# Third attention: value matrices as the stationary operand, two heads in the column halves of the array, probabilities scaled before they are turned

## The chip, the core and the metric

The program runs on one core of a Trainium2 chip. The core has five engines that run side by side, each in the order of its own instructions: TensorE (PE in the profile, with its weight loads as PEld), VectorE (DVE), ScalarE (ACT), GpSimd (POOL) and SyncE (SP, which only issues transfers here). They wait for each other by semaphores. The metric is the time of one execution in microseconds (us), as the median of several runs.

## The reference, cut to what matters

Two transformer blocks run one after the other on 256 tokens of width 1024. The change lies in the second block, in its mixer: 16 heads of width 64 in four groups of four (`moba`, `nsa`, `diff`, `swa`), each a softmax attention over 256 tokens with its own mask and slopes.

```python
p = _masked_softmax(sc, mask, sink)          # moba, slc, win, swa: one map for each head
o = jnp.einsum('bgrnqk,bgnkd->bgrnqd', p.astype(vb.dtype), vb)
...
return gates[..., 0:1] * o_c + gates[..., 1:2] * o_s + gates[..., 2:3] * o_w      # nsa
...
p = _masked_softmax(s1, mask) - lam * _masked_softmax(s2, mask)                   # diff
...
mix = jnp.concatenate([_merge(o_moba), _merge(o_nsa), _merge(o_diff), _merge(o_swa)], axis=-1)
x = x + _rms_norm(mix @ w_out[l], attn_post_norm[l])
```

At 256 tokens the selected and the windowed attention of `nsa` see all keys, so both are plain causal maps (`slc` and `win`). Everything is float32.

## The kernel before

**Matrix products with weights.** Weights arrive as float32 in slabs of two units (`raw`, three slabs). One unit is eight blocks of 128x128. Each unit is split into a high part (`wh`, rounded to fp32r) and a low part (`wl` = `raw` - `wh`), and a product is three fp32r matmuls. `MADE` gives each unit a letter that says who makes its parts: `d` low on VectorE and high on ScalarE, `p` low on GpSimd and high on ScalarE, `v` both on VectorE, `q` low on GpSimd and high on VectorE. A unit is made (`split`) some four units ahead of its use.

**Order.** All engines walk one list of steps, `ORDER`, and each issues only what it has to do in a step. The string `MIX["maps"]` weaves the third attention into the matrix products that it lies beside: a dot takes the next piece of the main chain (the projections `nkc`, `nq`, `d`, `s`, `mq`, `mk` of the second block, then the product `out2` with `w_out_2` in units `down`), a letter the next step of a job. Jobs are `a` (compressed keys and values), `b` and `c` (`slc` and `win`, by pairs of heads), `d` to `g` (the `df` maps), `h` and `i` (`swa`), `j` and `k` (`moba`).

**One pair of heads.** `scores` puts the two score maps side by side on the array, in its row halves. `score` (VectorE) adds the bias and takes the maximum, `exp` (ScalarE) makes unnormalised probabilities and their sums in a tile of `ringP` (seven tiles). `p_turn` transposes a map in three pieces of 128x128 on TensorE and ScalarE copies the 384 columns to a tile of `ringT` (five tiles). In `value` the turned probabilities are stationary and the 64 columns of V stream. `apart` does each of the three products in two column halves of the array: six instructions of 64 columns for one head. `o_out` (VectorE) multiplies the output by 1/sum (and by the gate for `nsa`) as it leaves PSUM, into `OM2`, token by head. For `nsa`, `cmp_value` multiplies the compressed probabilities `PcT` with their values, and VectorE adds.

**Joins.** Eight steps `join` transpose `OM2` back in two pieces of 128x128 each, and ScalarE (high) and VectorE (low) put the result into `mi`, the input of `out2`. `out2` reads `mi` in the order `KORD2` = 2, 3, 4, 5, 6, 7, 0, 1; the last four are in its `tail`. The `df` maps (`diff`) go through `d_mix`, `value`, `d_out`, `d_norm` and joins 4 and 5.

**Banks.** PSUM has eight banks; the steps of the attention take theirs in turn from five (`B5`). Every call of a matmul is issued by line 528, a transpose by 531, ScalarE by 534, VectorE by 537 to 555, GpSimd's copies by 564, transfers by 567.

Of the kernel before, what the change touches and what calls it, by code (L numbers as in the profile page):

```python
# [21 lines left out]
NUNREAD = 13  # L22
NBASE = 4
# [190 lines left out]
def segments():  # L214
# [163 lines left out]
    for n in range(2):  # L378
        jobs.append(two(("swa", n)) + ([("join", 6), ("join", 7)] if n else []))
    for n in range(2):  # L380
        jobs.append(two(("moba", n)) + [("join", n)])
# [27 lines left out]
    def names(steps):  # L409
# [12 lines left out]
        "ddvvvdvdppdpdppvvpdqpdpqvddpvpdvpdddvpdvpdvdddvqdddqqpddpddqddvdddddddpvvvdppvpppdvvddddqdvddddd"  # L422
        "dddddddddvdddvdpqpdddddddqddddddddddddddppddpddddddqddddvddvdvddddddpdvvdddvdvdddddd")
MIX = {
    "scan": "..abc.aabc..bb.c..ab.bc...a.b.b..cc...bcb.c..a..cc...bc.b.ca.bbcd.c..cbcbad.bd.c.e.b.ecf.ef.f.f.f",
    "latent": "..a......aaaaaaaa................bc....b.fgc.b..f.c.g..de.b.cf...d.gf.e.hi.dg.h.e.d..ie.h..i.h..i",
    "out1": "............c.caac..aaacabab.bbaaaaaa.baaabbbcbbbbbbbbccc....",
    "ffn1": "..aaaaac..acaba......aaaaaaaa....bbbbccbb......b.bbbb...bbbb............",
    "maps": "...a.....acbabcbc..cc.bbb.ede.eed.ecag.agcdgcggadc.b.bfcgbefdc.ab.dgfbe.dbhffbbhhhfa.ccccf.igecbeif."
            "gahf.ddib.b.bbigchijbjj..cbhcibchkhajkhcikkhcjbiijbcijkijkcijg.kjjkk.ggkkij.k.",  # L430
# [27 lines left out]
LAST_JOIN = [s for s in ORDER if s[0] == "join"][-1]  # L458
# [124 lines left out]
def program(nc, dr):  # L583
    ctx = ExitStack()
    with ctx:  # L585
# [184 lines left out]
        OM2 = fa(o, 2048).rearrange("p (c n) -> p c n", c=2); o += 2048  # L770
        PcT, VC = fa(o, 256), fa(o + 256, 256); o += 512
        ringP = [fa(o + 384 * i, 384) for i in range(7)]; o += 7 * 384
        ringT = [fa(o + 384 * i, 384) for i in range(5)]; o += 5 * 384
# [30 lines left out]
        HEAD = dict(moba=0, slc=4, win=4, df1=8, swa=12)  # L804
# [13 lines left out]
        for m, i in p_slot.items():  # L818
            p_prior[m] = at_p.get(i - 7)
        for m, i in t_slot.items():  # L820
            t_prior[m] = at_t.get(i - 5)
# [8 lines left out]
        def Pm(m):  # L830
            return ringP[p_slot[m] % 7]

        def Tm(m):
            return ringT[t_slot[m] % 5]
# [23 lines left out]
        def opened(e, u):  # L858
# [6 lines left out]
            elif PLACE[u] >= NBASE and OPENS[1] <= u < OPENS[1] + NWIDE - NBASE:  # L865
                e.wait_ge(*pe.at(LAST_JOIN))

# [14 lines left out]
        def tensor(e):  # L882
# [53 lines left out]
            for step in ORDER:  # L936
# [356 lines left out]
                elif kind == "p_turn":  # L1293
# [3 lines left out]
                    e.wait_ge(*(dve.at(("d_mix", m_[1])) if m_[0] == "df1" else act.at(("exp", m_))))  # L1297
# [3 lines left out]
                elif kind == "value":  # L1301
# [8 lines left out]
                    apart(b[:, 64:128], PT[:, 256:384], V[1], start=False).then_inc(*pe.up(step))  # L1310
                elif kind == "join":
# [4 lines left out]
                    for c in range(2):  # L1316
                        m = e.transpose(b[:, 128 * c:128 * c + 128], OM2[:, c, 128 * kt:128 * kt + 128], ident)
# [15 lines left out]
                elif kind in ("o_out", "d_out"):  # L1333
                    banks.give(("value", a[0] if kind == "o_out" else ("df1", a[0])))
# [18 lines left out]
                elif kind == "cmp_turn":  # L1353
# [4 lines left out]
                    m.then_inc(*pe.up(step))  # L1358
                elif kind == "cmp_value":
                    n, = a  # L1360
                    b = bank(step, B5)
                    e.wait_ge(*act.at("cmp_turn"))
                    e.wait_ge(*dve.at("cmp_kv"))
                    for c in range(2):
                        m = e.matmul(b[:, 128 * c:128 * c + 128], PcT[:, 128 * c:128 * c + 128], VC[:, 128 * n:128 * n + 128],
                                     start=True, stop=True)
# [3 lines left out]
        def scalar(e):  # L1370
# [3 lines left out]
            for step in ORDER:  # L1374
# [268 lines left out]
                elif kind == "p_turn":  # L1643
                    m_, = a
                    e.wait_ge(*pe.at(step))
                    if t_prior[m_]:
                        e.wait_ge(*pe.at(("value", t_prior[m_])))
# [843 lines left out]
```

## Time and profile before

| | us |
|---|---|
| median of 3 runs | 898.12 (897.7 to 898.27) |
| the profiled execution, its own time | 897.94 |
| span of its instructions | 896.1 |
| TensorE busy | 884.4 (99%) |
| TensorE weight loads busy | 782.7 (87%) |
| VectorE busy | 667.4 (74%) |
| ScalarE busy | 466.3 (52%) |
| GpSimd busy | 200.4 (22%) |

The page shows the clock of TensorE as full in all 40 slices. The chain that ended last is 96% TensorE. A busy figure of TensorE is not its peak: the end of a matmul is modelled, some 0.2 us after its last column went in, so short waits between matmuls are covered by the tail of the matmul before. What a step costs TensorE is therefore read from starts: from the start of its first row to the start of the next row of another kind. A fp32 matmul shows as two records (two passes), a transpose as one, a fp32r matmul as one. In a row of the trace, `128*64 128x64` is a stationary operand of 128 rows and 64 columns and a moving one of 64 columns.

### The profile page before, as it was taken

Reading aid. Unit: us, or ns where it says so; the run is one execution under the profiler, and the core shown is the slowest. Engines: PE = TensorE matmul, PEld = TensorE weight load, DVE = VectorE, ACT = ScalarE, POOL = GpSimd, SP = SyncE. Lnnn points to the kernel's source line nnn. Section 1 sums busy time; section 2 is a strip of 40 time slices with the busy share of each in tenths; the row PEclk is TensorE's granted clock in tenths of the full one; section 3 lists DMA queues with packets and bytes.
Section 4 is the critical chain, followed back from the end, with each engine's and each line's share of the span. In section 5 each row is a group of like instructions: output and inputs, shape, how many; then the busy total and the mean of one; then the engine's idle time right before and its main releaser. Section 6 shows DMA issues by size and latency. Waiting matters only on the chain.

```text
span 896.1 us, 16529 instructions
## 1 busy us (share of the span) xinstructions
PE 884.4 (99%) x6641; PEld 782.7 (87%) x6641; DVE 667.4 (74%) x1253; ACT 466.3 (52%) x940; POOL 200.4 (22%) x113
## 2 busy tenths in 40 slices
PE   9999999999999999999999999999999999999997
PEld 8879999989999798888888899977888888888886
DVE  7745987586447877786666767768888788788885
ACT  7444336665344774444444657866553545543443
POOL 4123421531132120553214522230001111210100
PEclk9999999999999999999999999999999999999999
DMA  8356453153424746555564374215354465465441
GB/s 331 114 184 234 140 174 112 48 212 142 142 96 145 278 163 236 188 196 187 187 219 169 124 247 165 97 48 211 142 222 161 182 213 204 152 230 188 174 156 48
DMA packets 23180, 153.66 MB, mean 171 GB/s; under 512 B 2864, under 2 KB 3248, under 8 KB 5568
## 3 DMA queue, kind: packets, MB, share of 16 engines
q1 hardware_dynamic: 22384, 150.44, 46.8%
q0 software_dynamic: 576, 2.10, 0.6%
q8 instruction: 53, 0.87, 0.4%
q14 instruction: 23, 0.19, 0.1%
q10 hardware_dynamic: 144, 0.07, 0.0%
HBM read 151.28 MB, written 1.05 MB: 170 GB/s over the span
## 4 chain that ended last, share of the span: by engine, by line
PE 96%; DVE 2%; ACT 1%; issue 1%; DVEq 0%; ACTq 0%
PE pb L528 94%; PE pb L531 2%; ACT FA L534 1%; DVE FA L537 0%; DVE wl L537 0%; ACT R L534 0%; DVE X L543 0%; DVE wh L552 0%; DVE FA L546 0%; ACT wh L534 0%; DVE FA L540 0%; DVE st L540 0%; DVE st L555 0%; DVEq L585 0%; DVE FA L543 0%
## 5 line engine op out<-in xcount | busy, mean ns | idle before, releaser
L528 PE MATMUL pb<-R,wh 128*128 128x256 f32 (+2 forms) x2224 | 545.5, 325 | 3.3 <-DVE R L543 2.0
L528 PE MATMUL pb<-R,wl 128*128 128x256 f32 (+1 forms) x1512 | 420.0, 281 | 0.0
L528 PEld LDWEIGHTS pb<-R,wh 128*128 128x128 f32 x2224 | 369.5, 188 | 43.3 <-ACT R L534 3.4
L537 DVE TENSOR_TENSOR wl<-raw,wh 128x1024 fp32r<-128x1024 f32 (+1 forms) x207 | 273.3, 1344 | 76.6 <-ACT wh L534 74.8
L537 POOL TENSOR_TENSOR wl<-raw,wh 128x1024 fp32r<-128x1024 f32 (+1 forms) x71 | 173.4, 2445 | 581.5 <-ACT wh L534 427.4
L528 PEld LDWEIGHTS pb<-R,wl 128*128 128x128 f32 x1512 | 283.4, 188 | 1.7
L534 ACT ACTIVATE wh<-raw 128x1024 fp32r<-128x1024 f32 (+1 forms) x223 | 226.1, 1044 | 52.0 <-PE pb L528 36.9
L528 PE MATMUL pb<-wh,R 128*128 128x512 f32 (+1 forms) x704 | 227.1, 389 | 0.1
L528 PEld LDWEIGHTS pb<-wh,R 128*128 128x128 f32 x704 | 131.7, 188 | 31.1 <-issue 1.7
L534 ACT ACTIVATE FA<-pb 128x256 f32<-128x256 f32 (+7 forms) x240 | 93.2, 411 | 118.4 <-PE pb L528 103.2
L528 PE MATMUL pb<-wl,R 128*128 128x512 f32 (+1 forms) x352 | 135.5, 385 | 0.0
L534 ACT ACTIVATE FA<-FA 128x256 f32<-128x256 f32 (+4 forms) x69 | 28.0, 406 | 138.9 <-DVE FA L543 118.8
L537 DVE TENSOR_TENSOR FA<-FA 128x256 f32<-128x256 f32 (+7 forms) x120 | 71.6, 621 | 10.1 <-ACT FA L534 2.9
L528 PEld LDWEIGHTS pb<-wl,R 128*128 128x128 f32 x352 | 66.1, 188 | 11.6
L537 DVE TENSOR_TENSOR FA<-pb,FA 128x256 f32<-128x256 f32 (+1 forms) x132 | 56.5, 434 | 24.8 <-ACT FA L534 24.3
L534 ACT ACTIVATE R<-FA 128x256 fp32r<-128x256 f32 (+1 forms) x66 | 28.3, 431 | 52.2 <-DVE FA L537 52.2
L528 PE MATMUL pb<-FA 128*32 128x16 f32 (+6 forms) x1360 | 54.0, 217 | 0.3 <-ACT FA L534 0.2
L528 PEld LDWEIGHTS pb<-FA 128*32 128x32 f32 (+3 forms) x1360 | 47.1, 130 | 7.2 <-issue 2.0
L552 DVE CAST wh<-raw 128x1024 fp32r<-128x1024 f32 (+1 forms) x55 | 42.3, 771 | 13.3 <-PE pb L528 12.7
L537 DVE TENSOR_TENSOR R<-FA,R 128x256 fp32r<-128x256 f32 (+1 forms) x59 | 27.4, 468 | 26.2 <-ACT R L534 26.1
L543 DVE SCALAR_TENSOR_TENSOR FA<-FA,sm 128x255 f32<-128x255 f32 x64 | 31.0, 484 | 2.3
L534 ACT ACTIVATE FA<-FA,st 128x256 f32<-128x256 f32 (+2 forms) x65 | 29.3, 454 | 5.2 <-DVE st L546 4.9
(127 smaller groups left out, 434.6 us busy)
## 6 DMA issues: line engine op xcount, KB each, us to landing
raw<-in_w SPq DMA_DIRECT2D x137, 1024.0 KB, 4.8
X<-in_x SPq DMA_DIRECT2D x2, 512.0 KB, 4.1
raw<-in_w SPq DMA_DIRECT2D x2, 512.0 KB, 6.8
post<-in_ffn_post SPq DMA_DIRECT2D x2, 512.0 KB, 4.3
post<-in_w POOLq DMA_DIRECT2D x2, 512.0 KB, 4.9
FA<-in_w POOLq DMA_DIRECT2D x2, 512.0 KB, 8.0
out<-X SPq DMA_DIRECT2D x4, 256.0 KB, 2.0
cst<-in_cst SPq DMA_DIRECT2D x1, 822.5 KB, 12.6
```

What stands on the lines that cost most here:

```text
L528: return self.real.matmul(*a, **k) if self.real else self
L531: return self.real.transpose(*a, **k) if self.real else self
L534: return self.real.activation(*a, **k) if self.real else self
L537: return self.real.tensor_tensor(*a, **k) if self.real else self
L543: return self.real.scalar_tensor_tensor(*a, **k) if self.real else self
L552: return self.real.tensor_copy(*a, **k) if self.real else self
```

## The change

- Each pair of heads of `slc`, `win`, `swa` and `moba` has one step `scale` after its two `exp` steps: VectorE makes 1/sum (times the gate) and multiplies the probabilities in `ringP` by it, two instructions for each map (128 and 256 columns). `p_turn` now waits for it.
- `value` of these 16 heads becomes `values` of 8 pairs. V (64 columns) is stationary and the turned probabilities stream, 256 columns and then 128. The first head of a pair takes the columns 0 to 63 of the array, the second 64 to 127. The output is head by token, as `mi` wants it. For `win` the compressed part is one matmul of 256 columns into the same bank ahead of the others, and `cmp_value` goes.
- `o_out` of a pair takes the output from PSUM to `mi` (ScalarE the high part, VectorE the low part); `slc` is first copied to `SLC` by ScalarE, and `win` adds it on VectorE. For `swa` the two parts are two instructions each of 64 partitions, since its pairs lie in two different parts of `mi`.
- Joins 0, 1, 2, 3, 6 and 7 go. 4 and 5 (`df`) stay. The `df` maps keep their `value`.
- The rings grow: `ringP` 12 tiles (7 before), `ringT` 7 (5 before). Space comes from `OM2`.
- `MIX["maps"]` is written anew, and 16 of the letters in `MADE`, all for units 157 to 182. High parts: seven fewer on ScalarE, seven more on VectorE. Low parts: six fewer on VectorE, six more on GpSimd.
- The buffers of the wide rings open after the last `values` and the `o_out` of `win`, no longer after the last join.

```diff
-        return [("scores", g), ("score", a), ("exp", a), ("score", b), ("exp", b), ("p_turn", a), ("value", a), ("p_turn", b), ("o_out", a),
-                ("value", b), ("o_out", b)]
+        return [("scores", g), ("score", a), ("exp", a), ("score", b), ("exp", b), ("scale", g), ("p_turn", a), ("p_turn", b), ("values", g),
+                ("o_out", g)]
...
-        jobs.append(two(("slc", n)) + two(("win", n)) + [("cmp_value", n), ("join", 2 + n)])
+        jobs.append(two(("slc", n)) + two(("win", n)))
...
-    "maps": "...a.....acbabcbc..cc.bbb.ede.eed.ecag.agcdgcggadc.b.bfcgbefdc.ab.dgfbe.dbhffbbhhhfa.ccccf.igecbeif."
...
+    "maps": ".....a...aabbcbcbcc..cb..dbee.deca.c.gegbadcaegdg..gcbfefcag.dfbd.e.bbhffbdhhghfbac.cfcg.cibgcef"
...
+                elif kind == "values":
+                    g, = a
+                    b = bank(step, B5, True)
...
+                    if g[0] == "win":
...
+                        e.matmul(b[:, 0:256], VC[:, 128 * g[1]:128 * g[1] + 128], PcT, start=True, stop=False)
+                    for c, t, k in ((0, slice(0, 256), slice(0, 256)), (1, slice(128, 256), slice(256, 384))):
+                        for m_ in GROUPS[g]:
+                            j = 64 * (m_[1] % 2)
+                            m = e.matmul(b[j:j + 64, t], MAPS[m_]["v"][c], Tm(m_)[:, k], start=c == 0 and g[0] != "win", stop=c == 1)
+                    m.then_inc(*pe.up(step))
...
+                elif kind == "scale":
+                    for m_ in GROUPS[a[0]]:
...
+                        e.reciprocal(r, stat(("sum", m_), 2)).then_inc(*dve.up())
...
+                    for m_ in GROUPS[a[0]]:
+                        S = Pm(m_)
+                        e.wait_ge(*dve.at(("r", m_)))
+                        for c in range(2):
+                            e.tensor_scalar(S[:, cols[c]], S[:, cols[c]], stat(("r", m_), 2)[:, c:c + 1], None,
+                                            ALU.mult).then_inc(*dve.up(("scaled", m_)))
```

TensorE at the end of the attention, from the last projection (`mk 1`, the rows `R,wh` and `R,wl`) to the first unit of `out2` (`wh,R`). `cst,FA` are transposes, `keys,FA` scores, `FA 64x64` the halves of a `value`, `FA 128x128` a `cmp_value`. Before:

```order
L528 MATMUL pb<-FA 64x64 x18
L531 MATMUL pb<-cst,FA 128x128 x9
L528 MATMUL pb<-keys,FA 128x128 x6
L531 MATMUL pb<-cst,FA 128x128 x2
L528 MATMUL pb<-FA 64x64 x18
L528 MATMUL pb<-FA 128x128 x2
L531 MATMUL pb<-cst,FA 128x128 x8
L528 MATMUL pb<-FA 128x128 x2
L528 MATMUL pb<-FA 64x64 x12
L531 MATMUL pb<-cst,FA 128x128 x10
L528 MATMUL pb<-wh,R 128x512
```

The same stretch of TensorE after the change; `FA 64x256` and `FA 64x128` are the two products of a head in `values`, `FA 128x256` the compressed part:

```order
L532 MATMUL pb<-FA 128x256
L532 MATMUL pb<-FA 64x256 x2
L532 MATMUL pb<-FA 64x128 x2
L535 MATMUL pb<-cst,FA 128x128 x6
L532 MATMUL pb<-keys,FA 128x128 x6
L535 MATMUL pb<-cst,FA 128x128 x3
...
L532 MATMUL pb<-FA 64x256 x2
L532 MATMUL pb<-FA 64x128 x2
L535 MATMUL pb<-cst,FA 128x128 x3
L532 MATMUL pb<-FA 64x256 x2
L532 MATMUL pb<-FA 64x128 x2
L535 MATMUL pb<-cst,FA 128x128 x6
L532 MATMUL pb<-wh,R 128x512
```

The 48 half products, four compressed products and 29 transposes of this stretch became 16 products of 64 stationary columns, two compressed ones and 18 transposes.

VectorE in the same place. Before, between the last two `score` steps of `moba` (`ISA`) and join 2 (`R<-pb,R`), it scales outputs of 64 columns out of PSUM (`pb`):

```order
L540 TENSOR_SCALAR FA<-pb,st 128x64 x2
L543 SCALAR_TENSOR_TENSOR FA<-pb,st,FA 128x64 x2
L537 TENSOR_TENSOR FA<-FA,pb 128x2x128
L537 TENSOR_TENSOR st<-st 128x2
L555 RECIPROCAL st<-st 128x2
L540 TENSOR_SCALAR FA<-pb,st 128x64 x2
L555 RECIPROCAL st<-st 128x2
L537 TENSOR_TENSOR R<-pb,R 128x256
```

After the change it writes the low parts of `swa`, scales the first pair of `moba` in SBUF and then adds and finishes the second pair of `win`:

```order
L541 TENSOR_TENSOR R<-pb,R 64x256 x2
L559 RECIPROCAL st<-st 128x2 x2
L544 TENSOR_SCALAR FA<-FA,st 128x128
L544 TENSOR_SCALAR FA<-FA,st 128x256
L544 TENSOR_SCALAR FA<-FA,st 128x128
L544 TENSOR_SCALAR FA<-FA,st 128x256
L541 TENSOR_TENSOR FA<-pb,FA 128x256
L541 TENSOR_TENSOR R<-FA,R 128x256
```

The multiplication by 1/sum moved from behind the value product to ahead of the transposes, and from PSUM to SBUF.

## Rows read from the trace of the kernel before

**Rows 1.** Page, part 1: busy us, share of the span, instructions.
```profile
PE 884.4 (99%) x6641; PEld 782.7 (87%) x6641; DVE 667.4 (74%) x1253; ACT 466.3 (52%) x940; POOL 200.4 (22%) x113
```
**Rows 2.** Stretches: from, to, length, busy of each engine, PEclk, DMA share, GB/s.
```profile
520.00:574.40 54.40, 54.18 (x606) 50.31 (x604) 39.34 (x157) 36.40 (x119) 12.17 (x10) 1.00 0.50 178
574.40:593.70 19.30, 18.32 (x234) 16.07 (x230) 13.29 (x70) 14.95 (x52) 4.68 (x2) 1.00 0.38 132
593.70:610.00 16.30, 16.30 (x109) 13.01 (x107) 10.60 (x30) 8.53 (x17) 2.39 (x1) 1.00 0.18 65
```
**Rows 3.** TensorE in order of time, start and length, around one `value`.
```profile
573.75 0.28 PE L528 MATMUL pb<-R,wl 128*128 128x256 f32 x1
573.95 0.57 PE L528 MATMUL pb<-FA 128*64 128x64 f32 x12
574.45 0.50 PE L528 MATMUL pb<-R,wh 128*128 128x256 f32 x2
574.79 0.28 PE L528 MATMUL pb<-R,wl 128*128 128x256 f32 x1
```
**Rows 4.** TensorE in order of time, last projection to first unit of `out2`.
```profile
583.41 1.27 PE L528 MATMUL pb<-FA 128*64 128x64 f32 x36
584.61 0.55 PE L531 MATMUL pb<-cst,FA 128*128 128x128 f32 x3
585.74 0.87 PE L531 MATMUL pb<-cst,FA 128*128 128x128 f32 x6 [0.58 <-ACT FA L534]
586.86 0.94 PE L528 MATMUL pb<-keys,FA 64*128 64x128 f32 x12 [0.25 <-ACT FA L534]
587.73 0.44 PE L531 MATMUL pb<-cst,FA 128*128 128x128 f32 x2
588.10 1.91 PE L528 MATMUL pb<-FA 128*64 128x64 f32 x40
589.85 1.18 PE L531 MATMUL pb<-cst,FA 128*128 128x128 f32 x8
591.17 1.56 PE L528 MATMUL pb<-FA 128*128 128x128 f32 x28
592.66 1.31 PE L531 MATMUL pb<-cst,FA 128*128 128x128 f32 x10
593.72 0.48 PE L528 MATMUL pb<-wh,R 128*128 128x512 f32 x1
```
**Rows 5.** TensorE in order of time: two `scores` steps between two `cmp_hid`.
```profile
531.75 1.61 PE L528 MATMUL pb<-keys,FA 64*128 64x128 f32 x24
533.29 0.64 PE L528 MATMUL pb<-FA 128*32 128x128 f32 x16
```
**Rows 6.** VectorE, groups by shape from 519 to 610 us: busy, mean ns.
```profile
L537 DVE TENSOR_TENSOR wl<-raw,wh 128x1024 fp32r<-128x1024 f32 x14 | 17.1, 1224 | 4.8 <-ACT wh L534 4.4
L540 DVE TENSOR_SCALAR FA<-pb,st 128x64 f32<-128x64 f32 x24 | 5.6, 277 | 0.2 <-PE pb L528 0.2
L540 DVE TENSOR_SCALAR FA<-FA,st 128x256 f32<-128x256 f32 x4 | 1.4, 349 | 0.0
L540 DVE TENSOR_SCALAR FA<-FA,st 128x128 f32<-128x128 f32 x4 | 1.1, 283 | 0.0
```
**Rows 7.** ScalarE, groups by shape from 519 to 610 us.
```profile
L534 ACT ACTIVATE wh<-raw 128x1024 fp32r<-128x1024 f32 x15 | 15.7, 1050 | 0.6 <-PE pb L528 0.6
L534 ACT ACTIVATE FA<-pb 128x384 f32<-128x384 f32 x20 | 9.2, 484 | 5.8 <-PE pb L531 5.8
```
**Rows 8.** GpSimd and VectorE in order of time, where a subtraction of GpSimd runs.
```profile
538.41 2.38 POOL L537 TENSOR_TENSOR wl<-raw,wh 128x1024 fp32r<-128x1024 f32 x1 [3.62 <-ACT wh L534]
583.32 4.68 POOL L537 TENSOR_TENSOR wl<-raw,wh 128x1024 fp32r<-128x1024 f32 x2 [9.58 <-ACT wh L534]
...
540.22 1.12 DVE L552 CAST wh<-raw 128x1024 fp32r<-128x1024 f32 x1 [3.86 <-PE pb L528]
544.66 0.69 DVE L552 CAST wh<-raw 128x1024 fp32r<-128x1024 f32 x1 [0.39 <-PE pb L528]
585.15 0.55 DVE L537 TENSOR_TENSOR st<-st 128x2 f32<-128x2 f32 x1
```

More of the change, by code:

```diff
@@ L22 @@
 NUNREAD = 13
+NTURN = 7
+NPROB = 12
 NBASE = 4
@@ L378, in segments @@
     for n in range(2):
-        jobs.append(two(("swa", n)) + ([("join", 6), ("join", 7)] if n else []))
+        jobs.append(two(("swa", n)))
     for n in range(2):
-        jobs.append(two(("moba", n)) + [("join", n)])
+        jobs.append(two(("moba", n)))
     segs.append(("maps", p.take(), jobs))
@@ L457 @@
     TAIL_AT.update({(_n, _k): BLOCK_AT["tail", _n] + 8 * _i for _i, _k in enumerate(_ks)})
-LAST_JOIN = [s for s in ORDER if s[0] == "join"][-1]
+LAST_READ = [s for s in ORDER if s[0] in ("join", "values")][-1]
 class Sig:
@@ L803, in program @@
                                   vs="tm2_out", sink=sc("sinks", h), less_sink=stat("less_sink", 4)[:, h:h + 1])
-        HEAD = dict(moba=0, slc=4, win=4, df1=8, swa=12)
+        KTILE = dict(moba=0, win=2, swa=6)
         def bias_of(m):
@@ L830, in Pm, with multiplied @@
         def Pm(m):
-            return ringP[p_slot[m] % 7]
+            return ringP[p_slot[m] % NPROB]
         def Tm(m):
-            return ringT[t_slot[m] % 5]
+            return ringT[t_slot[m] % NTURN]
+        def multiplied(m):
+            return ("value", m) if m[0] == "df1" else ("values", GROUP_OF[m][0])
         ALL = (0, 1, 2, 3, 4, 5, 6, 7)
@@ L1296, in tensor @@
                     S = Pm(m_)
-                    e.wait_ge(*(dve.at(("d_mix", m_[1])) if m_[0] == "df1" else act.at(("exp", m_))))
+                    if m_[0] == "df1":
+                        e.wait_ge(*dve.at(("d_mix", m_[1])))
+                    else:
+                        e.wait_ge(*dve.at(("scaled", m_)))
                     for i in range(3):
@@ L1333, in tensor @@
                 elif kind in ("o_out", "d_out"):
-                    banks.give(("value", a[0] if kind == "o_out" else ("df1", a[0])))
+                    banks.give(("values", a[0]) if kind == "o_out" else ("value", ("df1", a[0])))
                 elif kind == "cmp_act":
@@ L1357, in tensor @@
                         m = e.transpose(b[:, 128 * c:128 * c + 128], Sc_[:, 128 * c:128 * c + 128], ident)
[L1358 to L1366, printed above, removed]
                     m.then_inc(*pe.up(step))
@@ L1646, in scalar @@
                     if t_prior[m_]:
-                        e.wait_ge(*pe.at(("value", t_prior[m_])))
+                        e.wait_ge(*pe.at(multiplied(t_prior[m_])))
                     e.activation(Tm(m_), banks.of(step)[:, 0:384], ACT.Copy).then_inc(*act.up(step))
                     banks.ended(step, act.now())
+                elif kind == "o_out":
+                    (name, n), = a
+                    b = banks.of(("values", a[0]))
+                    e.wait_ge(*pe.at(("values", a[0])))
+                    if name == "slc":
+                        e.activation(SLC[n], b[:, 0:256], ACT.Copy).then_inc(*act.up(step))
+                        banks.ended(("values", a[0]), act.now())
+                    elif name == "win":
+                        e.wait_ge(*dve.at(("sum", n)))
+                        e.activation(operand("mi", 2 + n, 0), SLC[n], ACT.Copy).then_inc(*act.up(("mi", "h", 2 + n)))
+                    elif name == "moba":
+                        e.activation(operand("mi", n, 0), b[:, 0:256], ACT.Copy).then_inc(*act.up(("mi", "h", n)))
+                    else:
+                        for _, h in GROUPS[a[0]]:
+                            j = slice(64 * (h % 2), 64 * (h % 2) + 64)
+                            e.activation(operand("mi", 6 + h // 2, 0)[j, :], b[j, 0:256],
+                                         ACT.Copy).then_inc(*act.up(("mi", "h", 6 + h // 2), ("swa_h", h)))
                 elif kind == "d_out":
```

111 lines of the change are left out of this document (59 added, 52 removed).

## Prediction

> **What bounds the kernel now.** The page first: TensorE is busy 99% of the span, VectorE 74%, ScalarE 52%, GpSimd 22% [rows 1], and the granted clock is full in every stretch that the change touches [rows 2]. The chain that ended last is TensorE's. So a microsecond off TensorE's own work is a microsecond off the time, and work put on the others costs only where TensorE ends up waiting for it. The stretches [rows 2] show where that could be: over the first 54.4 us of the attention TensorE misses 0.22 us, since projections of 2.8 us each stand between the small steps. In the 19.3 us before `out2` it misses 0.98 us. After that nothing.
>
> The busy figure hides part of the waiting, so the end of the attention is read by starts [rows 4]: 10.31 us from 583.41 to 593.72. Price list from the same rows. Transposes: ten in 1.06 us, 0.106 each. A `value`: 0.50 us from its start to the next row [rows 3], and 36 records (three heads) take 1.20 us [rows 4], so 0.50 for the first of a run and 0.35 for each further one. A `cmp_value`: 588.10 to 589.85 is 1.75 us for three heads and one `cmp_value`, so 0.55. A `scores`: 0.87. The stretch holds eight heads in three runs (1.20 + 1.20 + 0.85), two `cmp_value` (1.10), 29 transposes (3.07) and one `scores` (0.87), together 8.3 us. The other 2.0 us are waits, of which the rows name 0.83, and drawn-out changes between kinds.
>
> **What TensorE loses and gains in work.** Removed: the 16 `value` steps. Before, they stand in ten runs, so 10 x 0.50 + 6 x 0.35 = 7.1 us. Two `cmp_value`: 1.1. Six joins of two transposes: 12 x 0.106 = 1.3. Together 9.5 us.
>
> Added: 8 `values`. No row shows 64 stationary columns with a long moving operand. The nearest is `scores`, which streams the same 384 columns for each of two maps, side by side in the row halves: 24 records in 1.54 us [rows 5], 0.77 each, or 0.87 alone [rows 4]. The lower bound of a `values` is that 0.77. The upper one is no overlap of the halves: 4 passes of 256 and 4 of 128 columns, at 0.106 for each 128 columns, 1.28 us. I take 0.90, close to `scores`, because the two halves of the array already overlap in `value` (36 records in 1.20 us are 0.033 us each, where 64 columns alone would be 0.053), and a little above it since passes of 256 and 128 columns alternate. 8 x 0.90 = 7.2. The compressed part is twice one matmul of 256 columns, two passes, 4 x 0.106 = 0.42, at most the 0.55 of `cmp_value`: 0.9 for both. Together 8.1 us. Net **-1.4 us** (bounds: 8 x 0.77 gives -2.4, 8 x 1.28 gives +1.6).
>
> On the uneven passes the Trainium skill (TensorE: Matmul & The Clock Gate, Part 3, The mechanism) says that matmuls start and end strictly in program order. By that, the first short pass of head A cannot end before the last long pass of head B, and a step would be 0.85 of streaming and some 0.1 to enter, 0.95; eight of them are 7.6 instead of 7.2, and the net would be -1.0. No row here shows unequal passes behind each other.
>
> **Changes of kind.** A lone `value` between two projections costs more than its 0.50: from the `wl` row at 573.75 to the one at 574.79 are 1.04 us where projections take 0.35 (24 of them in 2.83), so 0.69 [rows 3]. 0.19 is for going in and out. Ten runs become six (`slc` 1, `slc` 0, `win` 0, `win` 1 with `swa` 0, `swa` 1, `moba` 0 with 1): 4 x 0.18 = **-0.7 us**.
>
> **VectorE.** A scaled map is one instruction of 128 and one of 256 columns, 0.28 + 0.35 [rows 6], 16 x 0.63 = 10.1 us. It replaces two of 64 columns out of PSUM, 0.277 each, 16 x 0.55 = 8.9. The makers take 6 x 1.22 off it and give 7 x 0.69 [rows 6, 8]: -2.5. VectorE comes out even or 1 us lighter. ScalarE loses 7 x 1.05 = 7.4 us of high parts [rows 7] and gains two copies and two halves of some 0.4. GpSimd gains 6 x 2.4 = 14.4 us [rows 8], from a share of 22%. In sum no engine becomes the bound; what counts is order. All this is costed at nothing under the projections, 2.8 us of cover each.
>
> **Waits that come anew.** The way of a map was `exp`, `p_turn`, and is now `exp` of both heads, 1/sum, scaling, `p_turn`. Behind the waiting transposes stands everything else of TensorE. I walked the new order from the start of projection `mq 1` to `out2` by the same prices. (1) The transposes of `win` 0 stand right behind `mq 1`; ScalarE first has two pairs of `d_out` and two `exp` from the end of `mk 0`, then VectorE needs some 1.0 us for the factors and the first map. TensorE waits 0.8. (2) The transposes of `win` 2 wait for VectorE's next pair: 0.35. (3) `values` of `swa` 1 stands directly behind the last transposes that it needs, and the copy of 384 columns (0.48 [rows 7]) stands in ScalarE's queue behind two `exp` and the `o_out` of `swa` 0: 1.2. Together 2.3 us. Before, the same way from 574.45 held 2.0 us of slack after 583.41 and by the same count 0.5 ahead of it, so 2.5. These replace each other: 0, give or take 2 us. After `out2` has begun the new small steps each have a unit of 2.8 us ahead of them, as before. The deeper rings remove no wait that a row shows.
>
> The makers' change at the end (`out2`'s tail) takes one subtraction off VectorE and adds one cast, while TensorE is covered by the tail's four pieces: nothing.
>
> **Sum.** -1.4 - 0.7 + 0 = -2.1 us. Against the profiled execution 897.94 - 2.1 = 895.8; it lay 0.2 under the median of the runs shown, so **896.0**. A measurement of this kernel can tell about 0.2%, 1.8 us, from no change; 896.3 is that line.
>
> **Rivals.**
> (A) The waits go instead of being replaced. For it: fewer steps on TensorE for the same number of hand-overs (one `values` behind four copies, not four `value`), and ScalarE 7.4 us lighter in this segment. Then 2.3 us of my walk fall away: 893.6. Against it: the walk finds ScalarE and VectorE each close behind TensorE in three places.
> (B) The longer way of a map costs more than it saves: ScalarE or VectorE runs another 1.5 to 2 us late in the 19 us before `out2`, where VectorE was already busy 13.3 and ScalarE 15.0 of 19.3 us [rows 2]. Then 897.7, no change that can be told.
> (C) Slower: GpSimd's subtractions stop VectorE. While one ran from 538.41 to 540.79, a cast of VectorE that takes 0.69 took 1.12, and a 128x2 product took 0.55, ending with the first subtraction of the pair at 583.32 [rows 8]. Before, the scaling read PSUM. Now the 32 instructions read and write SBUF, and six more subtractions of 2.4 us run in the segment. Place: units 174 and 175, whose subtractions fall beside the scaling of `swa` 1 and `moba` 0. If two scalings are held for a whole subtraction, VectorE is 4.8 us late, TensorE has about 1 us of cover there: +3.8, 899.8. The time passes that of before once VectorE is 3.1 us late (2.1 + 1.0), 1.3 subtractions. Against it: most instructions of VectorE between two `split` steps read PSUM. In the walk the subtraction of 174 begins as the scaling of `swa` 1 ends.
> The Trainium skill (SBUF — State Buffer, Terms) states rival C as a rule: VectorE and GpSimd share a port pair that one holds for its full instruction while the other is blocked. The two rows agree with it for a cast and for a product of two SBUF operands; for a scaling out of SBUF no row shows it.
> (D) The halves do not overlap with long passes: 8 x 0.38 more, 899.0.
>
> **How the numbers follow.** Forecast (894.8 to 897.0) 0.42, of it 0.28 under 896.3. A 0.27. B 0.16. C 0.12. D 0.03. Faster by over 0.2%: 0.28 + 0.27 = 0.55. Within: 0.14 of the forecast and 0.13 of B, 0.27. Slower: C, D and the rest of B, 0.18. Range: down to A with `values` at its lower bound, 893.6 - 1.0 = 892.6; up to B and the nearer half of C and D, 899.0.
>
> **What the changed profile would show.** Right: `values` rows at 0.85 to 0.95 from start to start, 16 records or fewer each; TensorE busy some 2 us lower with idle in the segment about as before; the first unit of `out2` 17 to 18 us behind the start of `mq 1` (19.3 now). For A: idle rows of TensorE in the segment under 0.5 us in sum. For B: new idle ahead of transposes, put down to VectorE's scaling. For C: scalings that last 1 us or more while GpSimd subtracts. For D: `values` at 1.2 us or more. What would make all of it wrong is a difference outside the third attention, since the order there is the same.

## The result and the profile after

The changed kernel takes 902.55 us (median of 6 runs, 900.89 to 903.7), the kernel before 898.19 beside it (6 runs, 897.7 to 898.38): a ratio of 1.0046, interval 1.0033 to 1.0059. The prediction was 896.0 and faster. It was wrong in size and in sign.

The page of the changed kernel, part 1, against [rows 1]:
```profile
PE 882.9 (98%) x6497; PEld 779.1 (86%) x6497; DVE 675.6 (75%) x1256; ACT 461.3 (51%) x937; POOL 215.3 (24%) x119
```
TensorE is 1.5 us less busy, and the span is 4.6 us longer (900.7 against 896.1), so TensorE is idle 6.1 us more. VectorE is 8.2 us busier, where "even or 1 us lighter" was expected. The waits of TensorE from 495 to 640 us, by line and releaser (us in total, times, longest; three waits of 0.3 us and less left out):
```profile
PE pb L532 <- DVE st L544: 2.1, 1, 2.1
PE pb L535 <- DVE FA L544: 1.6, 1, 1.6
PE pb L532 <- ACT FA L538: 1.4, 2, 1.2
PE pb L532 <- DVE R L547: 1.1, 1, 1.1
PE pb L535 <- DVE st L550: 1.0, 1, 1.0
```
The lines have moved by a few: matmuls 532, transposes 535, ScalarE 538, VectorE 541 (two tensors), 544 (`tensor_scalar`), 550 (score), 556 (conversion), GpSimd's subtraction 541. The 1.1 stands behind the attention, and the kernel before has it too.

To find where the 4.6 us arise, the two traces are laid beside each other at two steps that both have: the transposes of `x3` for the second half of the tokens, ahead of the attention, and the first ones of `x4` behind it. Before:
```profile
507.29 1.04 PE L531 MATMUL pb<-cst,FA 128*128 128x128 f32 x8
...
619.24 1.03 PE L531 MATMUL pb<-cst,FA 128*128 128x128 f32 x8
```
After:
```profile
511.18 1.03 PE L535 MATMUL pb<-cst,FA 128*128 128x128 f32 x8
...
623.78 1.03 PE L535 MATMUL pb<-cst,FA 128*128 128x128 f32 x8
```
**3.9 us are lost before the attention has begun**, and 0.65 between the marks (112.60 against 111.95). Behind the second mark nothing more is lost.

**Ahead of the attention.** GpSimd, VectorE and TensorE of the changed kernel in order of time, where units 156 and 157 are made (157 is the one whose letter went from `d` to `p`):
```profile
503.11 2.52 POOL L541 TENSOR_TENSOR wl<-raw,wh 128x1024 fp32r<-128x1024 f32 x1 [2.25 <-ACT wh L538]
...
503.31 3.40 DVE L541 TENSOR_TENSOR wl<-raw,wh 128x1024 fp32r<-128x1024 f32 x1
506.63 0.14 DVE L544 TENSOR_SCALAR st<-st 128x1 f32<-128x1 f32 x1
...
506.86 0.77 PE L532 MATMUL pb<-wh,R 128*128 128x512 f32 x1 [2.15 <-DVE st L544]
507.42 0.63 PE L532 MATMUL pb<-wl,R 128*128 128x512 f32 x1
507.85 1.05 PE L532 MATMUL pb<-wh,R 128*128 128x512 f32 x2
```
And VectorE of the kernel before at the same place, which makes both units:
```profile
503.05 2.35 DVE L537 TENSOR_TENSOR wl<-raw,wh 128x1024 fp32r<-128x1024 f32 x2
505.32 0.15 DVE L540 TENSOR_SCALAR st<-st 128x1 f32<-128x1 f32 x1
```
One subtraction on VectorE beside one on GpSimd takes 3.40 us; two behind each other on VectorE take 2.35. What TensorE needs is the first of them, the low part of unit 156. In the kernel before it was done at 504.27 (503.05 and 1.22 of its own), and TensorE began with it at 504.41: there was no slack. Now it takes 2.18 us longer. TensorE waits 2.15 us, and then runs at half its clock. (The profile names the 128x1 product as the releaser, since it ends just behind the subtraction.) The stretches of after (busy of each engine, PEclk, DMA share, GB/s):
```profile
504.00:506.00 2.00, 0.71 (x4) 0.22 (x2) 2.00 (x1) 0.26 (x2) 1.92 (x2) 1.00 0.49 205
506.00:508.00 2.00, 1.14 (x3) 0.98 (x4) 1.42 (x4) 0.90 (x2) 1.92 (x2) 0.66 0.15 33
508.00:510.00 2.00, 2.00 (x7) 1.52 (x6) 0.00 (x0) 0.11 (x1) 1.92 (x3) 0.50 0.81 307
```
From 507.42 to 507.85, one record of 512 columns takes 0.43 us, where 0.23 is usual (502.68 to 502.91 in the same trace). 2.15 of waiting, some 1.4 of half clock and 0.3 by which this execution was already late make the 3.9. The half clock does not come in every execution. Of the six, two ended at 900.89 and 901.14 and four at 902.52 to 903.7, the profiled one among the four; the distance, some 1.4 us, fits the price of the half clock, though only one of the six was profiled.

**In the attention** TensorE waits 4.5 us by its rows, where before it waited 1.0. The three largest waits, with VectorE and GpSimd around them:
```profile
574.51 2.40 POOL L541 TENSOR_TENSOR wl<-raw,wh 128x1024 fp32r<-128x1024 f32 x1 [0.45 <-ACT wh L538]
578.68 2.38 POOL L541 TENSOR_TENSOR wl<-raw,wh 128x1024 fp32r<-128x1024 f32 x1 [1.77 <-DVE wh L556]
...
575.45 1.50 DVE L544 TENSOR_SCALAR st<-st 128x8 f32<-128x8 f32 x1
579.19 1.90 DVE L544 TENSOR_SCALAR st<-st 128x2 f32<-128x2 f32 x1
...
579.30 0.41 PE L535 MATMUL pb<-cst,FA 128*128 128x128 f32 x2 [1.00 <-DVE st L550]
584.18 0.52 PE L535 MATMUL pb<-cst,FA 128*128 128x128 f32 x3 [1.64 <-DVE FA L544]
596.75 0.87 PE L532 MATMUL pb<-FA 128*64 128x256 f32 x8 [1.24 <-ACT FA L538]
```
A product of 128x8 takes 1.50 us and one of 128x2 1.90, and each ends as GpSimd's subtraction ends (574.51 + 2.40, 578.68 + 2.38). "Held" is said below of an instruction of VectorE that takes that much longer beside a subtraction of GpSimd. The first reading was that both holds make a wait. Only one of them does, as the experiments show.

### The profile page after: what moved, and what is told of

Read it like the earlier page. It is cut to its first block, busy times and chain, and to the rows that moved or that the text cites. A ratio compares the mean times of both kernels' runs of the same rounds, so it can differ in the third digit from the quotient of the medians.

```text
span 900.7 us, 16249 instructions
## 1 busy us (share of the span) xinstructions
PE 882.9 (98%) x6497; PEld 779.1 (86%) x6497; DVE 675.6 (75%) x1256; ACT 461.3 (51%) x937; POOL 215.3 (24%) x119
## 3 DMA queue, kind: packets, MB, share of 16 engines
HBM read 151.28 MB, written 1.05 MB: 169 GB/s over the span
## 4 chain that ended last, share of the span: by engine, by line
PE 91%; DVE 4%; ACT 3%; issue 1%; DMA 1%; SPq 0%; DVEq 0%; ACTq 0%
PE pb L532 89%; ACT FA L538 2%; PE pb L535 2%; DVE wl L541 1%; DVE FA L541 1%; DMA X<-in_x 1%; ACT R L538 1%; DVE st L544 0%; DVE wh L556 0%; DVE X L547 0%; ACT L538 0%; DVE FA L544 0%; ACT wh L538 0%; DVE FA L550 0%; DVE st L559 0%
## 5 line engine op out<-in xcount | busy, mean ns | idle before, releaser
L541 POOL TENSOR_TENSOR wl<-raw,wh 128x1024 fp32r<-128x1024 f32 (+1 forms) x77 | 188.5, 2452 | 592.3 <-ACT wh L538 439.3
L541 DVE TENSOR_TENSOR wl<-raw,wh 128x1024 fp32r<-128x1024 f32 (+1 forms) x201 | 268.3, 1358 | 75.1 <-ACT wh L538 73.5
L538 ACT ACTIVATE wh<-raw 128x1024 fp32r<-128x1024 f32 (+1 forms) x216 | 219.1, 1044 | 55.1 <-PE pb L532 39.3
L556 DVE CAST wh<-raw 128x1024 fp32r<-128x1024 f32 (+1 forms) x62 | 48.1, 777 | 10.3 <-PE pb L532 10.2
L532 PE MATMUL pb<-FA 128*32 128x16 f32 (+10 forms) x1228 | 52.3, 221 | 1.4 <-ACT FA L538 1.4
L532 PEld LDWEIGHTS pb<-FA 128*32 128x32 f32 (+3 forms) x1228 | 44.1, 129 | 8.8 <-issue 2.4
```

What stands on the lines that cost most here:

```text
L532: return self.real.matmul(*a, **k) if self.real else self
L538: return self.real.activation(*a, **k) if self.real else self
L541: return self.real.tensor_tensor(*a, **k) if self.real else self
L556: return self.real.tensor_copy(*a, **k) if self.real else self
```

## The experiments

Each time is the median of 5 to 11 executions, with its ratio to the kernel before and the 95% interval. Beside them the kernel before ran at 898.03 (e1 to e4), 898.20 (e5 to e8), 897.96 (e9 to e11) and 898.26 us (e12, e13). Every `MADE[...]` line stands for one changed letter. Waits of single steps are those of the one profiled execution of each kernel, whose clock may have fallen or not. "Late" names a wait added to GpSimd, by this code in its `split`:
```
+                    if u in LATER:
+                        e.wait_ge(*dve.at(LATER[u]))
```

**e1: the changed kernel with unit 157 as before.**
```
+MADE[157] = "d"
```


> The changed kernel with one letter undone: unit 157 is a `d` again, so its low part is made by VectorE. Theory P (while GpSimd subtracts for 157, VectorE cannot run the subtraction for 156, which took 3.40 us instead of 1.2, and TensorE stands 2.15 us for it and then runs at half clock for some 3 us): the 3.6 us by which the changed kernel is behind at 511 us go, 902.6 - 3.6 = 899.0, still 0.8 above the kernel before. Rival W (the loss is made in the third attention and this place only shifts it): 902 or more. Rival Q (the waits in the attention are a consequence of the late start): 896 to 897.

898.97 us, 1.001 [1.0001, 1.0019]. The wait ahead of the attention is gone, and so is the half clock. 3.6 of the 4.4 us come back by one letter; by the two executions at 901, whose clock seems to have stayed, it would be some 2.0. What is left is 0.9 above before.

**e2: the same letter, alone, in the kernel before.**
```
+MADE[157] = "p"
```


> The kernel before with one letter changed: unit 157 is a `p`, low part on GpSimd. Theory P: 898.2 + 3.6 = 901.8, VectorE's subtraction for unit 156 at 3.4 us and a wait of TensorE of 2.1 us near 505. Rival W: 898.2, within 0.5.

900.98 us, 1.0036 [1.0024, 1.0049]: 2.9 us lost with nothing else changed. Its trace has the same 3.40 us subtraction and the same 2.15 us wait. In the profiled execution the clock stayed full, so its `x3` transposes come 2.45 us late and not 3.9. I had put the half clock into the sum as if it came every time. Three executions lie at 900.4 to 901.0 and two at 901.8 and 902.2.

**e4: e2 with GpSimd's subtraction behind VectorE's.**
```
+MADE[157] = "p"
-                    if u == BESIDE:
+                    if u in (BESIDE, 157):
                         e.wait_ge(*dve.at(("lo", u - 1)))
```


> As the kernel before with 157 on GpSimd, but GpSimd waits until VectorE has finished its subtraction for unit 156 before it begins that for 157. Theory P (the harm is that VectorE is held, not that GpSimd is slow): the subtraction for 156 takes 1.2 us again; 157 is then ready at about 506.7 where TensorE wants it at 506.1, and a 128x1 product of VectorE may still be held for up to 1.4 us: 898.7 to 900.0, under the run without the wait. Rival G (GpSimd's 2.4 us make unit 157 late): it gets later by this wait, 902.5 or more.

899.35 us, 1.0014 [1.0005, 1.0023]. GpSimd takes the same 2.38 us, later (from 504.24), and 1.6 of the 2.9 us are back. So the harm in e2 is mostly that two engines subtract at once. VectorE, then TensorE, of e4:
```profile
502.88 1.22 DVE L540 TENSOR_TENSOR wl<-raw,wh 128x1024 fp32r<-128x1024 f32 x1
...
504.58 0.17 DVE L558 RECIPROCAL st<-st 128x1 f32<-128x1 f32 x1 [0.42 <-ACT st L537]
504.78 2.12 DVE L543 TENSOR_SCALAR FA<-X,st 128x512 f32<-128x512 f32 x1
...
506.76 0.47 PE L531 MATMUL pb<-wh,R 128*128 128x512 f32 x1 [0.89 <-POOL wl L540]
```
The subtraction is back at 1.22, and now the scaling behind it is held (2.12, against 0.49 for the same instruction before). The reciprocal between them is not (0.17), though GpSimd is subtracting. Of the 1.3 us that are left, 0.89 is TensorE's wait for unit 157 itself, which GpSimd now makes too late: the rival of e4 has that part right.

**e3: the changed kernel with all sixteen old makers.**
```
+MADE[157] = "d"
+MADE[160] = "d"
...
+MADE[180] = "d"
+MADE[182] = "d"
```


> The changed kernel with all 16 letters of the makers as before the change; steps, values and scaling as changed. Theory P in full (GpSimd's subtractions for 171 and 173 also hold VectorE in the attention, a 128x8 product for 1.50 us and a 128x2 one for 1.90, and TensorE waits 1.0 and 1.64 for what follows): those two waits shrink, though VectorE has more to do and ScalarE 7.4 us more: 896.5 to 898.5, under the run with only 157 undone. Rival S (the waits come from the longer way exp, scaling, transposes and not from GpSimd): 899 or more, like the run with only 157 undone or slower, since ScalarE is fuller.

901.94 us, 1.0037 [1.0025, 1.005]: 3.0 above e1, although nothing is held ahead of the attention. Part of the 3.0 is half clock: the profiled execution has it from 579 to 582 us, and two of the five ended at 899.96 and 900.19, only 1.0 to 1.2 above e1. Even these are no faster than e1, so the new makers are not the whole fault. Unit 173 shows why (VectorE, then TensorE, of e3):
```profile
575.79 0.69 DVE L574 CAST wh<-raw 128x1024 fp32r<-128x1024 f32 x1
576.52 1.23 DVE L559 TENSOR_TENSOR wl<-raw,wh 128x1024 fp32r<-128x1024 f32 x1
577.66 0.28 DVE L568 CUSTOM_DVE_ANT_0 FA<-pb,FA 128x128 f32<-128x128 f32 x1
...
578.44 0.41 PE L553 MATMUL pb<-cst,FA 128*128 128x128 f32 x2 [2.26 <-DVE st L568]
```
With `v` VectorE converts and subtracts in front of a score, and TensorE waits 2.26 us where it waited 1.00. Another conversion (1.45 us, held) and subtraction run from 540.00 to 542.71 us in front of a scaling, and the transposes that need it wait 1.53. In these two places the new order is better off without VectorE's subtraction.

**e11: the kernel before with the fifteen new makers, without 157.**
```
+MADE[160] = "v"
+MADE[161] = "v"
...
+MADE[180] = "v"
+MADE[182] = "p"
```


> The kernel before with the fifteen new makers of the attention's units, without unit 157 (which e2 priced alone): the old products and the old order. If the makers only suit the new order and cost by themselves: 898.8 to 900.0, with holds where GpSimd has 171, 172, 173 one by one. If they are a gain for any order, by taking 1.05 us copies from ScalarE: 897.0 to 897.9. If nothing: 898.0 to 898.4.

899.09 us, 1.0011 [1.0002, 1.002], 1.1 above before. In the old order the same letters are a loss: a product of 128x2 takes 2.12 us under the subtraction of 173, and TensorE's waits in the segment go from 1.0 to 1.7.

**e5: e1 with unit 172's subtraction on VectorE.**
```
+MADE[157] = "d"
+MADE[172] = "d"
```


> The changed kernel with unit 157 back in the hands of VectorE (as in e1, 898.97 us) and unit 172 as well: VectorE makes its low part where GpSimd did at 571.18. Theory L (GpSimd's subtractions hold VectorE in front of the scaling): the 128x8 product takes 0.2 us again instead of 1.50, and the 1.22 us of the subtraction lie mostly in VectorE's 1.93 us of idle before 571.54; TensorE's wait in front of the compressed transposes goes from 1.00 to about 0.4, the second hold (1.90, by unit 173) stays. Time 898.0 to 898.6. Rival F (VectorE and ScalarE are simply full with scaling, exponentials and subtractions there, and a subtraction given to VectorE is one more piece in the row): 899.0 to 899.8.

903.83 us, 1.0068 [1.0055, 1.008]: 4.9 above e1, and neither theory had this. The 128x8 product takes 0.17 again, and something else costs the 4.9 us. VectorE and TensorE of e5:
```profile
570.99 1.23 DVE L545 TENSOR_TENSOR wl<-raw,wh 128x1024 fp32r<-128x1024 f32 x1 [2.65 <-ACT wh L542]
572.13 0.28 DVE L554 CUSTOM_DVE_ANT_0 FA<-pb,FA 128x128 f32<-128x128 f32 x1
...
572.92 1.65 PE L536 MATMUL pb<-keys,FA 64*128 64x128 f32 x12 [3.32 <-DVE st L554]
```
The idle that I had counted on was in front of the subtraction: VectorE waits 2.65 us for ScalarE's high part, and the scores queued behind it wait as well. TensorE waits 3.32 us, and is granted 0.50 of its clock from about 572 to 578.7:
```profile
569.00:573.00 4.00, 0.68 (x8) 0.51 (x6) 2.01 (x8) 2.30 (x9) 1.26 (x1) 0.85 0.41 123
573.00:576.00 3.00, 3.00 (x37) 2.66 (x37) 1.61 (x9) 1.34 (x9) 0.00 (x0) 0.50 0.47 191
576.00:580.00 4.00, 4.00 (x26) 4.00 (x24) 0.35 (x2) 1.03 (x5) 0.00 (x0) 0.67 0.00 0
```
With 172 on GpSimd, as in e1, no row of TensorE waits for it.

**e6: e1 with 173 late.**
```
+LATER = {173: ("scaled", ("swa", 1))}
```


> e1 (898.97 us) with one wait more: GpSimd's subtraction of unit 173 comes behind VectorE's scaling of the last sliding-window pair, at about 586 instead of 575.35 us. Its reader, the second block of the output projection, comes at 598. Theory L: the 128x2 product takes 0.23 instead of 1.90 us, the scores, exponentials and the scaling behind it come up to 1.7 us earlier, TensorE's wait of 1.64 in front of the first windowed transposes goes; the wait of 1.00 in front of the compressed ones stays: 897.3 to 897.8. Rival F: within 0.3 of 898.97, the wait only changes its releaser.

898.01 us, 1.0001 [0.9992, 1.001], 1.0 below e1, where 897.3 to 897.8 was expected. The wait of 1.64 is gone and the 128x2 product takes 0.23. Seven of the eleven runs lie at 897.5 to 898.2. The others, the profiled one among them, come at 898.9 to 899.4, and the profiled one shows 0.50 of the clock from 594 to 597:
```profile
584.00:592.00 8.00, 6.38 (x57) 4.20 (x56) 6.56 (x19) 6.42 (x20) 7.19 (x3) 1.00 0.40 134
...
594.00:597.00 3.00, 3.00 (x9) 2.33 (x9) 2.68 (x11) 2.92 (x6) 0.00 (x0) 0.50 0.46 194
```
The wait of 1.00 (compressed transposes) stays, and the one in front of the last `values` of `swa` goes from 1.24 to 1.58.

**e7: e5 and e6 together.**
```
+MADE[172] = "d"
+LATER = {173: ("scaled", ("swa", 1))}
```


> e5 and e6 together: unit 157 and 172 by VectorE, GpSimd's subtraction of unit 173 behind the scaling. Theory L: neither product is held; of the waits of 1.00 and 1.64 us about 0.3 is left: 896.4 to 897.1, which is the sum of the recorded prediction (896.0) with the wait in front of the last sliding-window product still there. Rival F: above 898.5.

903.02 us, 1.0054 [1.0042, 1.0067]. The 3.32 us wait of e5 is there again, with the half clock behind it (573 to 576), so the time does not test the sum. But the wait of 1.00 is there too, with both products unheld. By that the 128x8 hold isn't its cause.

**e8: e7 with the transposes of the last `swa` map earlier.**
```
+_x = ("p_turn", ("swa", 1))
+ORDER.remove(_x)
+ORDER.insert(ORDER.index(("values", ("win", 1))), _x)
```


> e7 with one step of the order moved as well: the transposes of the last sliding-window map stand in front of the products of the second windowed pair instead of directly in front of the product that reads them. Theory L: the wait of 1.24 us between these transposes and their product is a path of its own (transposes, ScalarE's copy, product) that about 2 us of other products now cover: 1.0 to 1.2 below e7, 895.2 to 896.1. Rival (ScalarE is behind with its queue there, so that the copy comes late wherever the transposes stand): the wait stays, within 0.3 of e7.

902.46 us, 1.0046 [1.0034, 1.0059], 0.6 below e7, where 1.0 to 1.2 was expected. Not all of the 0.6 is the moved step: the waits below differ by 0.2, and in the profiled execution of e8 (900.97) the clock stayed full although TensorE had waited the same 3.32 us. The wait of 1.58 falls to 0.61, but the one behind it rises from 0.25 to 1.00: the scaling of the first `moba` pair stands behind VectorE's share of the `swa` output.

**e9: e6 with 172 late as well.**
```
+LATER = {172: ("scaled", ("swa", 1)), 173: ("scaled", ("swa", 1))}
```


> e6 (unit 157 by VectorE, GpSimd's 173 behind the scaling; 898.01 us, 897.5 to 897.9 in the runs whose clock stayed) with unit 172 left to GpSimd but put behind the same scaling, which keeps it out of VectorE's queue: e5 gave it to VectorE, which then waited 2.65 us for ScalarE's high part with the compressed score queued behind it. Readers of 172 and 173 come at about 592 and 595. Theory L (holds are the loss): 128x8 product 0.2 instead of 1.50, the wait of 1.00 in front of the compressed transposes goes, and no 3.3 us wait appears: 896.5 to 897.1. Rival Q (VectorE's place in time there is set by its own queue and by ScalarE, the hold only fills idle): within 0.3 of e6. Rival B (four subtractions in a row hold the subtraction of the first windowed pair and the scaling of the first MoBA pair, and the output projection is late): 898.5 or more.

900.13 us, 1.0024 [1.0014, 1.0035], 2.1 above e6: rival B. The half clock is in it again: the profiled execution has it from 593 to 599 us, and four of the eight, without it by their times, lie at 899.1 to 899.5, some 1.4 above the seven faster ones of e6. The 128x8 product is free (0.17), and the wait of 1.00 stands unchanged, since VectorE's conversion behind the product then waits for TensorE instead. GpSimd now subtracts four times in a row, and the scaling is held. VectorE's conversion, then GpSimd, VectorE and TensorE at the scaling, of e9:
```profile
573.58 0.69 DVE L560 CAST wh<-raw 128x1024 fp32r<-128x1024 f32 x1 [1.16 <-PE pb L536]
...
583.54 9.50 POOL L545 TENSOR_TENSOR wl<-raw,wh 128x1024 fp32r<-128x1024 f32 x4 [14.07 <-DVE FA L548]
...
591.49 2.36 DVE L548 TENSOR_SCALAR FA<-FA,st 128x128 f32<-128x128 f32 x4
...
593.45 1.81 PE L539 MATMUL pb<-cst,FA 128*128 128x128 f32 x6 [1.16 <-DVE FA L548]
```

**e10: e9 with two steps moved.**
```
+for _x, _y in ((("p_turn", ("swa", 1)), ("values", ("win", 1))), (("scale", ("moba", 0)), ("values", ("win", 1)))):
+    ORDER.remove(_x)
+    ORDER.insert(ORDER.index(_y), _x)
```


> e9 with two steps moved in the order: the transposes of the last sliding-window map, and behind them the scaling of the first MoBA pair, in front of the products of the second windowed pair (e8 moved the first alone: the wait of 1.58 us went to 0.61, but 1.00 came at the MoBA transposes, whose scaling stood behind VectorE's part of the sliding-window outputs). Theory L: both waits go, 1.2 to 1.8 below e9, 895.0 to 895.8, which beats both kernels. Rival: the scaling is held by GpSimd's row of subtractions (583 to 592) and only moves the wait: within 0.4 of e9.

899.83 us, 1.0019 [1.001, 1.0027]: within 0.3 of e9, the rival. The moved scaling takes 3.91 us for the usual 1.0, under the same four subtractions. The wait of 1.59 falls to 0.61, and the one in front of the `moba` transposes grows from 1.16 to 1.76.

**e12: e6 with one score in front of a conversion.**
```
+for _x, _y in ((('score', ('swa', 2)), ('split', 173)),):
+    ORDER.remove(_x)
+    ORDER.insert(ORDER.index(_y), _x)
```


> e6 (898.01 us; 897.5 to 897.9 where the clock stayed) with one step of the order moved: VectorE's score of the second sliding-window map of the second pair stands in front of its conversion of unit 173 and no longer behind it. In e6, e8, e9 and e10 TensorE waits 1.00 us in front of the compressed transposes whether the 128x8 product is held (1.50) or not (0.2), so the hold isn't its cause. Theory Q: the conversion waits for TensorE to give up the buffer (1.16 us in e9), the score queued behind it frees the PSUM bank that the transposes take. With the score in front the wait of 1.00 goes: 896.5 to 897.2. Rival (the transposes wait for the compressed probabilities themselves): within 0.3 of e6.

897.16 us, 0.999 [0.9981, 0.9998], 0.85 below e6. Of this some 0.65 is the moved step, by the executions of both without the half clock (897.8 and 897.2 in the middle); the profiled one, 899.02, is the only one of eleven above 897.7, and has it. The wait of 1.00 falls to 0.37. VectorE, then TensorE, of e12; the scores (L557) now stand ahead of the conversion (L563):
```profile
574.39 0.28 DVE L557 CUSTOM_DVE_ANT_0 FA<-pb,FA 128x128 f32<-128x128 f32 x1
...
575.19 0.69 DVE L563 CAST wh<-raw 128x1024 fp32r<-128x1024 f32 x1
...
575.17 0.41 PE L542 MATMUL pb<-cst,FA 128*128 128x128 f32 x2 [0.37 <-DVE st L557]
```
So that wait was the maker's other half, the conversion that `q` gives to VectorE, in front of a score whose end frees a PSUM bank (the compressed transposes take theirs from the same five). What makes the rest of 0.37 wasn't tried.

**e13: e12 with two steps moved.**
```
+for _x, _y in ((('score', ('swa', 2)), ('split', 173)), (('p_turn', ('swa', 1)), ('values', ('win', 1))), (('scale', ('moba', 0)), ('o_out', ('swa', 0)))):
+    ORDER.remove(_x)
+    ORDER.insert(ORDER.index(_y), _x)
```


> e12 with two steps more: the transposes of the last sliding-window map in front of the products of the second windowed pair, and the scaling of the first MoBA pair in front of VectorE's part of the sliding-window outputs. GpSimd's three subtractions end at about 590 to 591 here, before that scaling begins, other than in e10 (four of them: 3.91 us for a scaling of 1.0). Expected: the wait of 1.58 falls to about 0.5 and the one of 0.25 stays under 0.4: 0.7 to 1.1 below e12, 895.5 to 896.4. If ScalarE's copies are what comes late there, the sum of the waits stays: within 0.3 of e12.

**896.45 us**, 0.998 [0.9971, 0.9989], 11 executions between 896.17 and 896.77, 0.7 below e12, and 1.8 below the kernel before. It is the fastest of all. From mark to mark it takes 110.45 us (507.29 to 617.74), before 111.95:
```profile
617.74 1.03 PE L542 MATMUL pb<-cst,FA 128*128 128x128 f32 x8
```
The clock stays full, and the wait of 1.58 falls to 0.61. The changed attention, fifteen new letters included, is worth 1.5 us between the marks once three steps stand elsewhere, one subtraction is late and the letter of unit 157 is taken back. No run gives the old products the same care, so how much of the 1.8 us is due to the new products alone isn't shown.

## Why the prediction was wrong

**The step that failed first** is the makers' term, costed at nothing "under the projections, 2.8 us of cover each", together with the prediction's last sentence, that the order outside the attention is the same. The order is the same, but a maker's letter moves an instruction between engines in an order that stands still. Unit 157 is made during the normalisation of `x3`, beside VectorE's subtraction for 156, which TensorE takes 0.14 us after its end. No projection covers it. I counted six subtractions less and did not place them one by one. In place of nothing the runs showed 3.9 us in the profiled execution, 2.9 us by medians when done alone (e2), 3.6 when undone (e1). The second step that failed is the waits in the attention, put at 0 and measured at 3.5 (below). Only the half clock in the 3.9 came by chance.

**The rows for it were there to be read.** Rival C had the mechanism right: GpSimd's subtraction holds instructions of VectorE that read and write SBUF. It had the place wrong. The trace of the kernel before even has the very case, two subtractions at once, GpSimd's and VectorE's:
```profile
371.89 2.40 POOL L537 TENSOR_TENSOR wl<-raw,wh 128x1024 fp32r<-128x1024 f32 x1 [1.76 <-ACT wh L534]
...
371.96 3.42 DVE L537 TENSOR_TENSOR wl<-raw,wh 128x1024 fp32r<-128x1024 f32 x1
```
All 19 subtractions of VectorE that begin there beside one of GpSimd take 1.6 to 3.4 us, for 1.22 alone. The scalings, for which I feared, are never held in the changed kernel: twenty of 256 columns take 348 ns in the mean and twenty of 128 take 280, as [rows 6] have them. Held were small steps in front of the scaling (two 128x2 products of `scale` steps among them, 2.39 us at 541.86 and 1.05 at 546.65, for which no row of TensorE waits), a conversion (2.17 us at 529.52) and a subtraction of VectorE ahead of it all. With the two of 128x8 and 128x2 shown above they are six, and took some 9.8 us more than such instructions take alone; before, it was two and 0.8 us. That is more than the 8.2 by which VectorE grew: the count of its work was about right, and its time was not. The Trainium skill (SBUF — State Buffer, Terms) says that one of the two engines holds the shared port pair for its full instruction while the other is blocked. The trace agrees: VectorE's 3.40 us are the 2.32 that were left of GpSimd's subtraction, and 1.08 behind its end, near the 1.22 of its own. I gave rival C 0.12, for two scalings, and priced it by where it would meet `scale` alone.

**TensorE's work: the term was mis-sized, to the good.** The rows of the new products are these (`values` of `slc` 1, of `win` 0 with its compressed part, and of `win` 1 and `swa` 0 in one run):
```profile
556.01 0.87 PE L532 MATMUL pb<-FA 128*64 128x256 f32 x8
556.81 0.55 PE L535 MATMUL pb<-cst,FA 128*128 128x128 f32 x3
...
589.61 1.40 PE L532 MATMUL pb<-FA 128*128 128x256 f32 x10
590.93 0.87 PE L535 MATMUL pb<-cst,FA 128*128 128x128 f32 x6
...
592.99 2.05 PE L532 MATMUL pb<-FA 128*128 128x256 f32 x18
594.97 0.55 PE L535 MATMUL pb<-cst,FA 128*128 128x128 f32 x3
```
A `values` (`slc` 0 and 1) is 0.80 from start to start, not 0.90, and with 1.32, 1.98, 0.81 and 1.52 for the rest all eight take 7.2 us where 8.1 was in the sum. From the strict order of starts and ends in the Trainium skill (TensorE: Matmul & The Clock Gate, Part 3, The mechanism) I had estimated 0.95. The trace does not bear the estimate out: 0.80 is under even its 0.85 of streaming. The halves do overlap, so rival D is out.

**Work and kinds together.** The segment is 0.65 longer with 3.5 us more of waits by the rows, so work and changes of kind are worth about -2.9, against -2.1 in the forecast. With -2.3 for the work (7.2 against the 9.5 removed, which was priced and not measured) some -0.6 is left for the kinds; -0.7 had been said. This is a remainder and not a reading. In e13, with 0.4 us more of waits than before, the same count gives -1.9: the waits of the rows are not the whole price of a wait, and the two terms can't be told apart to better than 1 us. Nor did the other sign appear, `out2` 17 to 18 us behind the start of `mq 1`: it is 19.2 in the changed kernel (19.3 before), and 17.0 in e13.

**Waits: "0, give or take 2" was 3.5.** Of the three foretold places one was right: the last `values` of `swa`, 1.24 against 1.2. The nearness is in part luck, since it becomes 1.58 in e6, when VectorE is not held. The transposes of `win` 0 waited 1.64 and not 0.8, since GpSimd's subtraction of 173 held VectorE; without the hold they wait nothing (e6). The transposes of `win` 2 waited nothing. Not foretold was 1.00 in front of the compressed transposes, from a conversion that `q` puts on VectorE ahead of a score (e12). I had walked the queues with durations and not with the places of the `split` steps. And the 2.5 us of "old waits" that these were to replace are 1.0 by rows: I had put drawn-out changes between kinds into it, which the new kernel has as well.

**The sum** of the profiled executions: -2.9 work and kinds, +3.5 waits, +3.9 ahead of the attention, 4.5 us, which is what the spans differ by. It closes by construction, as the first term is a remainder; read from the trace are the 3.9, the 0.65 between the marks and the waits.

**Still open.** How often the half clock comes, and what decides it: its share in the median of the changed kernel is known only by the two groups of times (some 1.4 us).

## What to carry to other kernels

When a change hands work between two engines that share something, place every instruction handed over in the order of both and ask what stands beside it and behind it. A saving counted by engine does not tell the price: one letter out of sixteen cost 2.9 us, and giving a subtraction back to VectorE cost 4.9, because it waited at the head of an in-order queue. And when an order has been woven for one set of costs, look for the steps that stand directly behind what they wait for, or behind something long that others don't need yet. Three moved steps and one late subtraction turned 0.9 us over (e1) into 1.8 under (e13).

## What the runs showed of the hardware

- A subtraction of 128x1024 on GpSimd (2.4 us) holds many instructions of VectorE that have all operands in SBUF, small ones too: products of 128x8 took 1.50 for 0.17, of 128x2 1.90 for 0.23, of 128x512 2.12 for 0.49 (e4), four scalings 3.91 for 1.0 (e10).
- It does not hold all of them. Beside such a subtraction a reciprocal of 128x1 took its usual 0.17 (504.58 in e4), one of 128x2 0.16 (546.46 in the changed kernel), a reduction of 128x120 0.27 (575.14), a product of 128x1 0.14 (500.53). Scores that read PSUM kept their 0.28 and 0.42.
- Two subtractions at once, one on each engine, end later (VectorE's after 3.40 us) than two in a row on VectorE (2.35).
- TensorE's granted clock fell to 0.50 (1.2 of 2.4 GHz) for some 3 to 7 us in single executions, and no one wait decides it. After a wait of 2.15 us it fell in the profiled execution of the changed kernel, and not in that of e2. After 3.32 us it fell in e5 and e7, and not in e8. It also fell in e6 with no wait over 1.58, after 8 us in which TensorE was busy 6.4, while seven of its eleven executions were over 0.7 us faster.
